# Three of the four low parts of each head's output weights made by GpSimd instead of VectorE

## Chip, cores and metric

The kernel runs on one core of a Trainium2 chip. The metric is the device time of one execution in microseconds (us); lower is better.

## What is computed

One inference step of a two-layer trunk: layer 0 is sliding-window attention, layer 1 an mLSTM block, for a prompt of 1024 tokens (with 16 meta tokens ahead of it) and for 8 short samples of 4 tokens. The change lies in the second layer. Per head (4 heads of width 512) the prompt goes through a chunkwise recurrence, here shortened to its shape:

```
def step(carry, xs):                      # one chunk of one head
    C, n, m = carry                       # C: 512 x 512 state
    s = einsum('td,jd->tj', qc, kc) * w_intra
    num = s @ vc + w_inter * (qc @ C)
    den = sum(s, axis=j) + w_inter * (qc @ n)
    h = num / max(abs(den), exp(-m_t))
    C_new = decay * C + (kc * wk).T @ vc
    n_new = decay * n + sum(wk * kc)
...
h_norm = (h - mean(h)) * rsqrt(var(h) + eps) * head_norm
y = ((sigmoid(o) * h_norm + skip * xc) * silu(z)) @ w_out
```

The sum over heads in `@ w_out` is made head by head: each head adds its 512 rows of `w_out` times its 512 gated channels to the output.

## The kernel before

After a first stage (projections) the kernel runs the cell stage, from about 1612 us to the end, head after head. The text calls the heads 0 to 3; head 0 and head 3 are written out with constants, heads 1 and 2 are two turns of one hardware loop, whose waits use registers. A head has chunks 0 to 8 of the prompt (chunk 0 has the 16 meta tokens, the others 128 each) and one set of samples. Each engine has its own program (`cell_pe`, `cell_dve`, `cell_act`, `cell_gp`, `cell_sp`) and they meet only by semaphores; the order on each engine is written out by hand.

In a chunk `c` TensorE (PE) transposes keys and values (`pre`, L1564), multiplies queries by the state (L1635), makes the rest of the numerator (L1646), then the state's update (L1653). VectorE (DVE) copies the denominator out (L1943), works on it in three tiny instructions (`denominator`, L1853 to L1855), adds the four quarters of the update to the state `cst` (`prompt_state`, L1872), takes the statistics and makes the normed output `hb` (`normed`, L1879 and L1880), which PE transposes (`back`, L1582). PE's update and DVE's addition alternate over two banks of `ps`, so each can hold up the other. From chunk 2 on DVE also updates one sample's state per chunk (`sample_state`, L1811). GpSimd (POOL) makes gates, key weights, queries times weight (`queries`, L1480) and, last in a chunk, one sample's keys (`sequence_keys`, L1498).

The output product at a head's end (`out_part`, L1678) multiplies in single passes, so each weight is split in a high part `whi` (by ScalarE, `w_high`, L1757) and a low part `wlo = wraw - whi`. The head's weights come in four pieces of 128x1024 over three buffers. Their low parts were made by DVE in `w_low` (L1895): pieces 0 to 2 between the sample updates and the denominator of chunks 1 to 3, piece 3 amid the output product, once piece 0's buffer is free. The loads of the pieces, in `cell_sp`, wait on the same semaphore `o_lo` that counts low parts.

Of the kernel before, what the change touches and what calls it, by code (L numbers as in the profile page):

```python
# [20 lines left out]
F32 = mybir.dt.float32  # L21
F32R = mybir.dt.float32r
ALU = mybir.AluOpType
# [25 lines left out]
KT = D // P  # L49
# [48 lines left out]
def due(n):  # L98

    n = n.v if isinstance(n, Idx) else n  # L100
    return max(n, 0) if isinstance(n, int) else n


def wait_apart(eng, sem, n):


    n = n.v if isinstance(n, Idx) else n
    if not isinstance(n, int):
        n = eng.to_reg(n)
        eng.wait_ge(sem, 1)  # L110
    eng.wait_ge(sem, due(n))
# [21 lines left out]
def build(nc, a, o):  # L133
# [3 lines left out]
    def sem(name):  # L137
        if name not in sems:
            sems[name] = nc.alloc_semaphore(name + sem_suffix[0])
        return sems[name]  # L140
# [3 lines left out]
    def sb(name, shape, off, dt=F32):  # L144
        assert BASE + off + 4 * int(np.prod(shape[1:])) <= 229368, name
        return nc.alloc_sbuf_tensor_at("sb_" + name, shape, dt, offset=BASE + off)
# [40 lines left out]
    wraw = [sb(f"wraw{i}", [P, KT * P], WB + i * SLOT) for i in range(NSLOT)]  # L187
    whi = [sb(f"whi{i}", [P, KT * P], WB + (NSLOT + i) * SLOT, F32R) for i in range(NSLOT)]
    wlo = [sb(f"wlo{i}", [P, KT * P], WB + (2 * NSLOT + i) * SLOT, F32R) for i in range(NSLOT)]
# [1139 lines left out]
    def pre_no(c):  # L1329

        return 0 if c == NCH - 1 else c + 1

    def used(h, c):

        return NU * h + (u_tile(c - 2, 3) + 1 if c > 1 else 0)
# [8 lines left out]
    def turn_of(h, c):  # L1344

        return 5 * h + c // 2 if c % 2 == 0 else 4 * h + c // 2
# [101 lines left out]
    def cell_gp(gp, h):  # L1448
        def exponents(c):

            n = ROWN[c]
            if c == NCH - 1:
                gp.wait_ge(sem("head_set"), 4 * h + 4)
                gp.tensor_tensor(ees[:, :], habs[:, :], trism[:, :], ALU.add).then_inc(sem("e_ready"), 1)
                return
            gp.wait_ge(sem("abc_in"), 16 * h + 16)
            gp.wait_ge(sem("w_done"), NCH * h + pre_no(c) - 1)
            if c > 1:
                gp.wait_ge(sem("u_add"), NCH * h + c - 1)
            else:  # L1460
                gp.wait_ge(sem("qs_ready"), NCH * h + pre_no(c))
            gp.tensor_tensor(ee[c % 2][0:n, 0:n], abc[0:n, COL0[c]:COL0[c] + n], tri[0:n, 0:n], ALU.add)\
                .then_inc(sem("e_ready"), 1)

        def queries(c):

            n = ROWN[c]
            if c == NCH - 1:
                gp.wait_ge(sem("smin"), 144 * h + 144)
                w, dst = hws[:, :], qss  # L1470
            else:
                gp.wait_ge(sem(f"chin{c % 2}"), 48 * turn_of(h, c) + 48)
                gp.wait_ge(sem("wint"), NP * h + c + 1)
                gp.wait_ge(sem("u_ready"), used(h, c))
                w, dst = wnt[c % 2][:, 0:n], qs[c % 2]
            if c in (NCH - 1, 0):
                gp.wait_ge(sem("e_ready"), NCH * h + pre_no(c) + 1)
            else:
                gp.wait_ge(sem("kwt_ready"), NP * h + c)
            gp.tensor_tensor(dst[:, :, 0:n], chunk_in(c)[:, 0, :, 0:n],  # L1480
                             w.rearrange("p (a t) -> p a t", a=1).to_broadcast([P, 4, n]), ALU.mult)\
                .then_inc(sem("qs_ready"), 1)

        def spread_queries():

            wait_apart(gp, sem("qs_ready"), NCH * h + 1)
            wait_apart(gp, sem("sn_full"), h)
            gp.tensor_copy(diagonal(qz), qss[:, :, :].rearrange("p k (b t) -> p b k t", b=DECB)).then_inc(sem("qz_ready"), 1)

        def sequence_keys(b):  # L1490

            wait_apart(gp, sem("k3_lo"), 2 * h + 1)
            if b < DECB - 1:
                wait_apart(gp, sem("qs_ready"), NCH * h + pre_no(b + 2) + 1)
            else:
                wait_apart(gp, sem("kwt_ready"), NP * h + NP)
            wait_apart(gp, sem("u_ready"), samp_used(h, b))
            gp.tensor_scalar(kwz[b % 2][:, :], k3[:, :].bitcast(F32), blkm[0:SR, b:b + 1], None, ALU.mult).then_inc(sem("kwz_ready"), 1)  # L1498

        def gated(c):  # L1500

            n, u = ROWN[c], ub[c % 2]
            gb = gates_of(c)[1]
            wait_gates(gp, h, c)
            gp.wait_ge(sem("u_mul"), NCH * h + c + 1)
            gp.tensor_tensor(u[:, :, 0:n], u[:, :, 0:n], gb[:, :, 0:n], ALU.add).then_inc(sem("u_add"), 1)

        def put_low(c):

            n, u = ROWN[c], ub[c % 2]  # L1510
            gp.wait_ge(sem("uh_done"), NCH * h + c + 1)
            cols = slice(COL0[c], COL0[c] + n)
            gp.tensor_tensor(ul[:, :, cols], u[:, :, 0:n], uh[:, :, cols].bitcast(F32), ALU.subtract).then_inc(sem("ul_done"), 1)  # L1513

        def weighted_keys(c):

            n = ROWN[c]
            gp.wait_ge(sem(f"chin{c % 2}"), 48 * turn_of(h, c) + 48)
            gp.wait_ge(sem(f"chw{c % 2}"), 16 * turn_of(h, c) + 16)
            if c == 0:  # L1520
                gp.wait_ge(sem("num9"), h)
            else:
                gp.wait_ge(sem("ns_ready"), NP * h + c)
            gp.tensor_tensor(kwt[:, :, 0:n], chin[c % 2][:, 1, :, 0:n],
                             chw[c % 2][:, 0:n].rearrange("p (a t) -> p a t", a=1).to_broadcast([P, 4, n]), ALU.mult)\
                .then_inc(sem("kwt_ready"), 1)

        exponents(NCH - 1)
        queries(NCH - 1)
        spread_queries()  # L1530
        exponents(0)
        queries(0)
        for c in range(NP):
            if c >= 1:
                gated(c - 1)
            if c + 1 < NP:
                exponents(c + 1)
            weighted_keys(c)
            if c >= 1:
                put_low(c - 1)  # L1540
            if c + 1 < NP:
                queries(c + 1)
            if c >= 1:
                sequence_keys(c - 1)
        gp.wait_ge(sem("kwz_ready"), DECB * h + DECB)
        for c in (NP - 1, NCH - 1):
            gated(c)
            put_low(c)

    def cell_pe(pe, h):  # L1550
# [131 lines left out]

        pe.wait_ge(sem("ul_done"), NCH * h + NP)
        pe.wait_ge(sem("c_done"), NU * h + NU)
        pe.wait_ge(sem("o_lo"), 4 * h + 1)
        out_part(0, (0, 1))
        out_part(1, (0, 1))
        back(NCH - 1)
# [2 lines left out]
        for i in range(2):  # L1691
            out_part(i, (2,)).then_inc(sem("o_full"), 1)
        for i in range(2, KT):
            pe.wait_ge(sem("o_lo"), 4 * h + i // 2 + 1)
            pe.wait_ge(sem("o_done"), KT * h + i - 1)
            out_part(i, (0, 1, 2)).then_inc(sem("o_full"), 1)

# [83 lines left out]
    def cell_dve(dve, h):  # L1781
# [108 lines left out]
            dve.tensor_tensor(u[:, :, 0:n], pm[1][:, :].rearrange("p (k t) -> p k t", k=4)[:, :, 0:n], ga[:, :, 0:n], ALU.mult)\  # L1890
                .then_inc(sem("u_mul"), 1)

        def w_low(j):
            dve.wait_ge(sem("o_hi"), due(4 * h + j + 1))
            dve.tensor_tensor(wlo[j % 3][:, :], wraw[j % 3][:, :], whi[j % 3][:, :].bitcast(F32), ALU.subtract)\  # L1895
                .then_inc(sem("o_lo"), 1)


        if isinstance(h, int) and h == 0:
# [25 lines left out]
        for c in range(NP):  # L1925
            n, r = ROWN[c], c % 2
            if c == 0:
                dve.wait_ge(sem("cst_out"), 16 * h)
            if c > 0:
                put(c - 1)  # L1930
            score_low(c)
            value_low(c)
            if c > 1:
                sample_state(c - 2, 0)
                sample_state(c - 2, 1)
            key_low(c)
            if c > 1:
                sample_state(c - 2, 2)
                sample_state(c - 2, 3)
            if 0 < c < 4:  # L1940
                w_low(c - 1)
            small(c + 1)
            done(dve.tensor_copy(cs[0:n, r, 0:1], SM[0:n, 0:1]))  # L1943
            dve.sem_inc(sem("small_read"), 1)
            denominator(c)
            prompt_state(c, 0)
            prompt_state(c, 1)
            statistics(c)
            prompt_state(c, 2)
            prompt_state(c, 3)  # L1950
            normed(c)
            if c + 1 < NP:
                scores(c + 1)
            key_state(c)
# [15 lines left out]
        for i in range(KT):  # L1970
            dve.wait_ge(sem("o_full"), KT * h + i + 1)
            dve.tensor_tensor(v3(x1T[:, i, :]), ps[i % 2][:, :, 0:GRP], v3(x1T[:, i, :]), ALU.add).then_inc(sem("o_done"), 1)  # L1972
            if i == 1:
                w_low(3)
        dve.wait_ge(sem("o_done"), KT * h + KT)
        assert step[0] == CELL_STEPS, step[0]

# [554 lines left out]
```

## Time and profile before

| | |
|---|---|
| time, median of 3 runs | 2410.4 us (2406.17 to 2413.91) |
| profiled execution: its time, its span | 2409.14 us, 2407.4 us |
| PE busy, share of span | 2197.8 us, 91% |
| DVE busy | 1120.1 us, 47% |
| ACT busy | 711.0 us, 30% |
| POOL busy | 497.0 us, 21% |
| DVE `wlo` in the cell stage (L1895), 16 of them | 24.1 us, 1504 ns each |

Shares of busy time are means over stages with different limits. In the timeline a row has the start, the duration and what ended the engine's idle time before it. Granted clock 1.00 is TensorE's 2.4 GHz level and 0.50 its 1.2 GHz level.

### The profile page before, as it was taken

To read this page: it belongs to the slowest core of one execution; us is meant where nothing else is said; L and a number is where in the kernel's file an instruction comes from. 1 tells how busy PE (TensorE), PEld (TensorE's weight loads), DVE (VectorE), ACT (ScalarE), POOL (GpSimd) and SP (SyncE) were. 2 spreads that over 40 slices of the span, in tenths; PEclk is the share of its full clock that TensorE was granted. 3 is DMA by queue.
4 is the path that set the end of the run, shared out by engine and by line. 5 is a ranking of instruction groups with operands and counts; after the bars stand their busy time and mean duration, and the time that the engine had idled before them with its cause. 6 is when DMAs were issued, how large, how long until landed. Compare 5 with 4: busy or idle time off the path is not lost. (4 is left out here: it accounts for less than half of the span.)

```text
span 2407.4 us, 34739 instructions
## 1 busy us (share of the span) xinstructions
PE 2197.8 (91%) x12991; PEld 1902.7 (79%) x12991; DVE 1120.1 (47%) x1906; ACT 711.0 (30%) x1497; POOL 497.0 (21%) x464
## 2 busy tenths in 40 slices
PE   5999979968999999999999999928998998999997
PEld 4999967737999989998998999815686676667667
DVE  6222348733554305512451354037736844853863
ACT  3115658821133313322332232113303312311320
POOL 3000026601420001100010010004503512521430
PEclk8999979957999999999999999968998988988999
DMA  6621021002331332232123222237853861754661
GB/s 207 83 79 36 27 61 51 1 26 96 118 90 63 118 109 63 81 127 83 63 81 136 74 82 98 84 80 236 254 167 91 254 178 54 244 173 121 192 203 74
DMA packets 307072, 268.43 MB, mean 112 GB/s; under 512 B 60642, under 2 KB 252610, under 8 KB 306831
## 3 DMA queue, kind: packets, MB, share of 16 engines
q1 hardware_dynamic: 293034, 217.48, 30.2%
q10 hardware_dynamic: 13880, 48.77, 6.2%
q8 instruction: 109, 1.79, 0.3%
q14 instruction: 49, 0.40, 0.1%
HBM read 164.75 MB, written 102.40 MB: 111 GB/s over the span
## 5 line engine op out<-in xcount | busy, mean ns | idle before, releaser
L380 DVE TENSOR_TENSOR sb_wlo<-sb_wraw,sb_whi 128x1024 fp32r<-128x1024 f32 x100 | 143.2, 1432 | 278.8 <-ACT sb_whi L375 272.1
L396 PE MATMUL ps<-sb_h1h,sb_whi 128*128 128x360 f32 x1152 | 253.7, 328 | 3.8 <-issue 3.8
L375 ACT ACTIVATE sb_whi<-sb_wraw 128x1024 fp32r<-128x1024 f32 x100 | 105.7, 1058 | 512.8 <-PE ps L396 443.4
L396 PE MATMUL ps<-sb_h1l,sb_whi 128*128 128x360 f32 x1152 | 252.5, 327 | 0.0
L396 PE MATMUL ps<-sb_h1h,sb_wlo 128*128 128x360 f32 x1152 | 252.2, 327 | 0.0
L396 PEld LDWEIGHTS ps<-sb_h1h,sb_whi 128*128 128x128 f32 x1152 | 198.9, 188 | 6.5 <-issue 6.3
L396 PEld LDWEIGHTS ps<-sb_h1h,sb_wlo 128*128 128x128 f32 x1152 | 199.7, 188 | 0.0
L396 PEld LDWEIGHTS ps<-sb_h1l,sb_whi 128*128 128x128 f32 x1152 | 199.4, 188 | 0.0
L948 POOL COPY sb_ctail<-sb_xr 128x3 f32<-128x3 f32 (+1 forms) x16 | 3.0, 188 | 708.4 <-DVE sb_xr L1081 708.4
L1635 PE MATMUL pm<-sb_cst,sb_qs 128*128 128x512 f32 x256 | 135.5, 611 | 1.0 <-issue 0.9
L396 PE MATMUL ps<-sb_hh,sb_whi 128*128 128x360 f32 x480 | 117.4, 353 | 15.8 <-DVE sb_hl L417 12.6
L1054 ACT ACTIVATE sb_st<-ps 128x1080 f32<-128x1080 f32 x48 | 51.5, 1072 | 226.8 <-PE ps L396 226.8
L1811 DVE SCALAR_TENSOR_TENSOR sb_scs<-sb_scs,sb_hbc,ps 128x512 f32<-128x512 f32 x128 | 94.4, 744 | 29.8 <-PE ps L1591 29.7
L396 PE MATMUL ps<-sb_hl,sb_whi 128*128 128x360 f32 x480 | 107.4, 333 | 0.0
L396 PE MATMUL ps<-sb_hh,sb_wlo 128*128 128x360 f32 x480 | 106.7, 331 | 0.0
L396 PEld LDWEIGHTS ps<-sb_hh,sb_whi 128*128 128x128 f32 x480 | 85.5, 194 | 24.8 <-issue 9.8
L1678 PE MATMUL ps<-sb_uh,sb_whi 128*128 128x360 f32 x384 | 92.7, 336 | 11.8 <-POOL sb_ul L1513 11.8
L1972 DVE TENSOR_TENSOR sb_x1T<-ps,sb_x1T 128x1080 f32<-128x1080 f32 x32 | 41.1, 1283 | 127.8 <-PE ps L1678 127.8
L1638 PEld LDWEIGHTS ps<-sb_nst,sb_qs 128*128 128x128 f32 x256 | 48.9, 191 | 62.6 <-issue 62.6
L1678 PE MATMUL ps<-sb_uh,sb_wlo 128*128 128x360 f32 x384 | 91.3, 332 | 0.0
L1678 PE MATMUL ps<-sb_ul,sb_whi 128*128 128x360 f32 x384 | 91.1, 332 | 0.0
L1872 DVE SCALAR_TENSOR_TENSOR sb_cst<-sb_cst,sb_hbc,ps 128x512 f32<-128x512 f32 x128 | 89.4, 739 | 0.6 <-issue 0.6
(394 smaller groups left out, 4726.6 us busy)
## 6 DMA issues: line engine op xcount, KB each, us to landing
sb_scs<-state_mlstm_c SPq DMA_DIRECT2D x32, 1024.0 KB, 5.5
sample_mlstm_c<-sb_scs SPq DMA_DIRECT2D x32, 1024.0 KB, 4.4
sb_wraw<-mlstm_w_in SPq DMA_DIRECT2D x48, 512.0 KB, 3.8
sb_wraw<-swa_w_in SPq DMA_DIRECT2D x20, 512.0 KB, 3.8
scratch_ga<-sb_st ACTq DMA_DIRECT2D x16, 540.0 KB, 2.7
scratch_gb<-sb_st ACTq DMA_DIRECT2D x16, 540.0 KB, 3.7
scratch_v<-sb_st ACTq DMA_DIRECT2D x16, 540.0 KB, 2.7
scratch_q<-sb_st ACTq DMA_DIRECT2D x16, 540.0 KB, 2.7
```

The costliest lines, as they stand in the source:

```text
L375: act.activation(whi[q][:, :], wraw[q][:, :], ACT.Copy).then_inc(sem("w_hi"), 1)
L380: dve.tensor_tensor(wlo[q][:, :], wraw[q][:, :], whi[q][:, :].bitcast(F32), ALU.subtract)\
L396: last = pe.matmul(ps[s][:, g, 0:GRP], w[:, kk, c * P:(c + 1) * P], x[:, kk, g * GRP:(g + 1) * GRP], start=(kk == 0 and i == 0), stop=(kk ...
L948: gp.tensor_copy(dst[:, 0:CW - 1], x[:, NPR:XPR])
L1054: act.activation(v3(st[b][:, 0, :]), ps[c][:, :, 0:GRP], ACT.Copy, scale=(MD ** -0.5 if i // 4 == 2 else 1.0)).then_inc(sem("qkv_ev"), 1)
L1635: pe.matmul(pm[0][0:n, :], qs[r][:, k, 0:n], cst[:, k, :], start=(k == 0), stop=False)
L1638: pe.matmul(SM[0:n, 0:1], qs[r][:, k, 0:n], nst[:, k:k + 1], start=(k == 0), stop=False)
L1678: last = pe.matmul(ps[i % 2][:, g, 0:GRP], w[:, k, c * P:(c + 1) * P], x[:, k, g * GRP:(g + 1) * GRP], start=(k == 0 and t == 0), stop=(k ...
L1811: dve.scalar_tensor_tensor(scs[b % 2][:, k, :], scs[b % 2][:, k, :], hbc[:, 1, NP + b:NP + b + 1], U_[u % 2], ALU.mult, ALU.add).then_inc( ...
L1872: ins = dve.scalar_tensor_tensor(cst[:, k, :], cst[:, k, :], hbc[:, 1, c:c + 1], U, ALU.mult, ALU.add)
L1972: dve.tensor_tensor(v3(x1T[:, i, :]), ps[i % 2][:, :, 0:GRP], v3(x1T[:, i, :]), ALU.add).then_inc(sem("o_done"), 1)
```

## The change

GpSimd makes pieces 0 to 2 at the end of its chunks 1 to 3, DVE keeps piece 3, and PE waits for three low parts at once before the output product.

```diff
@@ cell_gp
+        def weight_low(j):
+            wait_apart(gp, sem("o_hi"), 4 * h + j + 1)
+            wait_apart(gp, sem("o_full"), KT * h)
+            gp.tensor_tensor(wlo[j][:, :], wraw[j][:, :], whi[j][:, :].bitcast(F32), ALU.subtract).then_inc(sem("o_lo"), 1)
...
             if c >= 1:
                 sequence_keys(c - 1)
+            if c in (1, 2, 3):
+                weight_low(c - 1)
@@ cell_pe
-        pe.wait_ge(sem("o_lo"), 4 * h + 1)
+        pe.wait_ge(sem("o_lo"), 4 * h + 3)
...
         for i in range(2, KT):
-            pe.wait_ge(sem("o_lo"), 4 * h + i // 2 + 1)
+            if i == 6:
+                pe.wait_ge(sem("o_lo"), 4 * h + 4)
@@ cell_dve
-        def w_low(j):
-            dve.wait_ge(sem("o_hi"), due(4 * h + j + 1))
-            dve.tensor_tensor(wlo[j % 3][:, :], wraw[j % 3][:, :], whi[j % 3][:, :].bitcast(F32), ALU.subtract)\
-                .then_inc(sem("o_lo"), 1)
+        def last_low():
+            dve.wait_ge(sem("o_hi"), 4 * h + 4)
+            dve.wait_ge(sem("o_lo"), 4 * h + 3)
+            dve.tensor_tensor(wlo[0][:, :], wraw[0][:, :], whi[0][:, :].bitcast(F32), ALU.subtract).then_inc(sem("o_lo"), 1)
...
-            if 0 < c < 4:
-                w_low(c - 1)
...
             if i == 1:
-                w_low(3)
+                last_low()
```

On POOL, chunk 1 of head 0, the order before is this (L1480 are the queries of chunk 2, L1498 the sample's keys; `sb_kwz` is their tile):

```order
L1524 TENSOR_TENSOR sb_nums<-sb_chin_191,sb_headsum 128x512
L1513 TENSOR_TENSOR sb_ul<-sb_ub_243,sb_uh 128x4x16
L1480 TENSOR_TENSOR sb_qs_228<-sb_chin_190,sb_wnt_212 128x512
L1498 ISA
L1498 TENSOR_SCALAR sb_kwz_236<-sb_k_232,sb_blkm 96x512
L1506 TENSOR_TENSOR sb_ub_244<-sb_ub_244,sb_chga_193 128x512
```

and this is what stands there now:

```order
L1524 TENSOR_TENSOR sb_nums<-sb_chin_191,sb_headsum 128x512
L1513 TENSOR_TENSOR sb_ul<-sb_ub_243,sb_uh 128x4x16
L1480 TENSOR_TENSOR sb_qs_228<-sb_chin_190,sb_wnt_212 128x512
L1498 ISA
L1498 TENSOR_SCALAR sb_kwz_236<-sb_k_232,sb_blkm 96x512
L1531 TENSOR_TENSOR sb_wlo_71<-sb_wraw_65,sb_whi_68 128x1024
L1506 TENSOR_TENSOR sb_ub_244<-sb_ub_244,sb_chga_193 128x512
```

One instruction came in, between the sample's keys and the gate (L1506) that opens the next chunk on POOL.

On DVE, chunk 2 of head 0, before (L1811 adds to a sample's state, L1943 opens the denominator):

```order
L1811 SCALAR_TENSOR_TENSOR sb_scs_205<-sb_scs_205,sb_hbc,ps 128x512 x2
L1818 SCALAR_TENSOR_TENSOR sb_kl_220<-ps,sb_hcol,sb_kh_218 128x512
L1811 SCALAR_TENSOR_TENSOR sb_scs_205<-sb_scs_205,sb_hbc,ps 128x512 x2
L1895 TENSOR_TENSOR sb_wlo_72<-sb_wraw_66,sb_whi_69 128x1024
L1943 COPY sb_cs<-ps 128x1
L1853 SCALAR_TENSOR_TENSOR sb_cs<-sb_cs 128x1
L1854 TENSOR_TENSOR sb_cs<-sb_cs,sb_hcol 128x1
```

and now (the same lines stand 6 to 8 lines further down in the file):

```order
L1819 SCALAR_TENSOR_TENSOR sb_scs_205<-sb_scs_205,sb_hbc,ps 128x512 x2
L1826 SCALAR_TENSOR_TENSOR sb_kl_220<-ps,sb_hcol,sb_kh_218 128x512
L1819 SCALAR_TENSOR_TENSOR sb_scs_205<-sb_scs_205,sb_hbc,ps 128x512 x2
L1949 COPY sb_cs<-ps 128x1
L1861 SCALAR_TENSOR_TENSOR sb_cs<-sb_cs 128x1
L1862 TENSOR_TENSOR sb_cs<-sb_cs,sb_hcol 128x1
```

The low part left the place ahead of the denominator; nothing else moved.

## Rows read from the trace of the kernel before

**Rows 1.** Chain that ended last, head 2, chunk 3: start, us, piece

```profile
2063.00 0.94 DVE sb_cs L1853
```

**Rows 2.** Timeline of DVE, head 2: start, us, instruction, [idle before <-releaser]

```profile
2029.47 1.98 DVE L1895 TENSOR_TENSOR sb_wlo<-sb_wraw,sb_whi 128x1024 fp32r<-128x1024 f32 x1
2033.80 0.16 DVE L1943 COPY sb_cs<-ps 128x1 f32<-128x1 f32 x1 [2.34 <-PE pm L1646]
2034.10 0.16 DVE L1853 SCALAR_TENSOR_TENSOR sb_cs<-sb_cs 128x1 f32<-128x1 f32 x1
...
2047.07 1.51 DVE L1895 TENSOR_TENSOR sb_wlo<-sb_wraw,sb_whi 128x1024 fp32r<-128x1024 f32 x1
...
2063.00 0.93 DVE L1853 SCALAR_TENSOR_TENSOR sb_cs<-sb_cs 128x1 f32<-128x1 f32 x1
...
2068.32 0.15 DVE L1879 TENSOR_TENSOR sb_cs<-sb_cs 128x1 f32<-128x1 f32 x1
...
2076.77 0.16 DVE L1943 COPY sb_cs<-ps 128x1 f32<-128x1 f32 x1 [0.17 <-PE pm L1646]
...
2116.28 0.16 DVE L1943 COPY sb_cs<-ps 128x1 f32<-128x1 f32 x1 [0.17 <-PE pm L1646]
```

**Rows 3.** Timeline of POOL (GpSimd), head 2, chunks 1 to 3

```profile
2028.20 0.32 POOL L1506 TENSOR_TENSOR sb_ub<-sb_ub,sb_chga 128x64 f32<-128x64 f32 x1 [13.75 <-DVE sb_ub L1890]
...
2030.33 1.30 POOL L1513 TENSOR_TENSOR sb_ul<-sb_ub,sb_uh 128x64 fp32r<-128x64 f32 x1
...
2033.02 1.56 POOL L1498 TENSOR_SCALAR sb_kwz<-sb_k,sb_blkm 96x512 fp32r<-96x512 f32 x1 [0.16 <-POOL sb_qs L1480]
...
2047.66 2.35 POOL L1498 TENSOR_SCALAR sb_kwz<-sb_k,sb_blkm 96x512 fp32r<-96x512 f32 x1 [0.16 <-POOL sb_qs L1480]
...
2061.67 2.25 POOL L1480 TENSOR_TENSOR sb_qs<-sb_chin,sb_wnt 128x512 f32<-128x512 f32 x1 [0.88 <-DMA sb_chin<-scratch_v]
2064.22 1.56 POOL L1498 TENSOR_SCALAR sb_kwz<-sb_k,sb_blkm 96x512 fp32r<-96x512 f32 x1 [0.31 <-POOL sb_qs L1480]
```

**Rows 4.** Timeline of PE, head 2, behind the third low part

```profile
2065.20 0.50 PE L1653 MATMUL ps<-sb_vh,sb_kh 128*128 128x512 f32 x1 [2.05 <-DVE sb_cst L1872]
```

**Rows 5.** Groups of POOL instructions by shape: xcount | busy us, mean ns

```profile
L952 POOL TENSOR_TENSOR sb_xml<-sb_xr,sb_xmh 128x1040 fp32r<-128x1040 f32 x16 | 41.5, 2594 | 0.0
```

**Rows 6.** Timelines of POOL and DVE, chunk 1 of heads 0, 1 and 3

```profile
1651.10 1.57 POOL L1498 TENSOR_SCALAR sb_kwz<-sb_k,sb_blkm 96x512 fp32r<-96x512 f32 x1 [0.17 <-issue]
...
1651.83 0.16 DVE L1854 TENSOR_TENSOR sb_cs<-sb_cs,sb_hcol 128x1 f32<-128x1 f32 x1
...
1836.98 1.56 POOL L1498 TENSOR_SCALAR sb_kwz<-sb_k,sb_blkm 96x512 fp32r<-96x512 f32 x1 [0.16 <-POOL sb_qs L1480]
...
1839.96 0.16 DVE L1853 SCALAR_TENSOR_TENSOR sb_cs<-sb_cs 128x1 f32<-128x1 f32 x1
...
2224.55 1.56 POOL L1498 TENSOR_SCALAR sb_kwz<-sb_k,sb_blkm 96x512 fp32r<-96x512 f32 x1 [0.16 <-issue]
...
2225.12 0.16 DVE L1853 SCALAR_TENSOR_TENSOR sb_cs<-sb_cs 128x1 f32<-128x1 f32 x1 [0.15 <-DVE sb_cs L1943]
```

**Rows 7.** Timelines of DVE and PE, head 3, chunks 3, 4 and 7

```profile
2252.83 0.15 DVE L1943 COPY sb_cs<-ps 128x1 f32<-128x1 f32 x1
...
2255.14 0.50 PE L1653 MATMUL ps<-sb_vh,sb_kh 128*128 128x512 f32 x1 [1.84 <-DVE sb_cst L1872]
...
2268.01 0.16 DVE L1943 COPY sb_cs<-ps 128x1 f32<-128x1 f32 x1 [0.17 <-PE pm L1646]
...
2306.42 0.16 DVE L1943 COPY sb_cs<-ps 128x1 f32<-128x1 f32 x1 [0.17 <-PE pm L1646]
```

**Rows 8.** Windows of 1 us, head 3: busy us (x) of PE, PEld, DVE, ACT, POOL, granted clock, DMA

```profile
2257.00:2258.00 1.00, 1.00 (x6) 0.94 (x5) 1.00 (x2) 0.41 (x2) 0.00 (x0) 0.50 0.25 45
```

**Rows 9.** Timelines of PE and POOL, head 2, inputs of chunk 8

```profile
2119.50 1.03 PE L1564 MATMUL ps<-sb_ident,sb_chin 128*128 128x128 f32 x8
...
2119.51 1.28 POOL L1480 TENSOR_TENSOR sb_qs<-sb_chin,sb_wnt 128x512 f32<-128x512 f32 x1 [4.28 <-DMA sb_chin<-scratch_v]
```

## Prediction

> **What bounds the kernel now.** I read the page first: PE is busy for 91% of the span, but that is a mean over stages, and the change touches only the cell stage, four heads of some 195 us. So I read the chain that ended last there. It hops between PE and DVE in every chunk: PE's query and update products, then DVE's denominator and the first quarter of the state, then PE's update again. One of its pieces is a DVE instruction on a 128x1 column that takes 0.94 us [rows 1]. The timeline of DVE tells why that is odd. The reader is to see three things in it [rows 2]. First, in chunk 1 DVE makes a low part (2029.47, 1.98 us) and then idles 2.34 us until PE ends the numerator: that low part costs the chain nothing. Second, the denominator's copy L1943 gives the beat of the chunks: 2076.77 to 2116.28 is three chunks without low part, 39.51 us or 13.17 each; 2033.80 to 2076.77 is three that hold the second and third low part, 42.97 us. Third, L1853 takes 0.16 us at 2034.10 and 0.93 at 2063.00, behind the third low part. The timeline of POOL gives the reason [rows 3]: POOL's queries began at 2061.67, took 2.25 us instead of 1.28 [rows 9] and ended at 2063.92; L1853 ended at 2063.93. DVE's low part and POOL's product kept each other out, and then POOL kept DVE's tiny instruction out until its own end. In chunk 1 it is the same the other way: POOL's L1513 on 64 columns took 1.30 us beside DVE's low part, where L1506 on as many took 0.32 [rows 3]. So two engines share something when both read two tensors from SBUF. L1872, L1811 and the statistics read one tensor there and the other in PSUM, and show no such lengthening. This is what the change has to be judged by, since it puts the longest such instruction on POOL.
>
> **What it removes.** Per head, 3.46 us at most (42.97 - 39.51) [rows 2]; at least the 1.51 us of the second low part plus the 0.77 us that L1853 lost (0.93 - 0.16), 2.28 us. In chunk 2 of heads 1 and 2 the sample's keys L1498 now start right at the denominator (2047.66 [rows 3] against 2047.07 plus L1943 and L1853), and L1854, with two tensors in SBUF, will meet them. How long L1498 keeps others out is bounded by head 3: L1853 starts 0.57 us behind the start of L1498 and takes 0.16 [rows 6], so for less than 0.57 us. I take 0.4 of that off and get 3.1 us per head, 12.4 in all (the written-out heads 0 and 3 lose less there, but have shorter chunks).
>
> The Trainium skill, "SBUF — State Buffer", section "Who interferes with whom", says that whichever of the two engines starts first gets the shared pair "for the whole instruction". For L1498, with one tensor input, head 3's row says otherwise: L1853 would have had to wait a microsecond there. By the page the sum would come out about 2 us higher, 2409; by the row it stays.
>
> Heads 0 and 3 have one more thing to get back. PE waits 1.84 us behind the third low part, and the granted clock then falls to 0.50, the 1.2 GHz level [rows 7, 8]. L1943 to L1943 takes 15.18 us there; in head 2 the same stretch is 14.07 (2063.00 less 0.30 to 2076.77 [rows 2]), and head 3's plain chunk is 12.80 (2268.01 to 2306.42, three of them [rows 7]), 0.37 shorter than head 2's. So the fall costs 15.18 - 14.07 + 0.37 = 1.5 us. Heads 1 and 2 had the longer wait (2.05 [rows 4]) without a fall. With the wait gone, two falls go: 3.0 us. Gross gain: 15.4 us.
>
> **What it adds.** A 128x1024 subtraction of two SBUF tensors on POOL. The nearest row is L952, same form, 1040 columns, 2.59 us [rows 5]; for 1024, 2.55 us. POOL has room for it: it follows L1498 (kwz), and POOL's next gate waits for DVE, so at the end of its own chunk it delays nobody on POOL. But for 2.4 us (until some 0.15 us before its end, since L1853, 0.16 us long, ended together with L1480 above) DVE can't run L1853, L1854, L1879 or L1840, all with two SBUF tensors. So the question is where these fall.
>
> Chunk 1: without DVE's low part beside it, L1513 takes 0.32 instead of 1.30, and all behind it on POOL moves up 0.98. In head 2, L1498 goes from 2033.02 to 2032.04, ends at 2033.6 [rows 3], and the low part runs from 2033.6 to 2036.1. PE's numerator hasn't moved, so L1853 comes at 2034.10 [rows 2], is kept out until 2036.0 and delays the first quarter of the state, for which PE waits: 1.9 us on the chain. In head 0, L1498 moves from 1651.10 to 1650.12 and the low part starts at 1651.66; L1854 comes at 1651.83 [rows 6]: it loses by 0.17 us and waits 2.2. Head 3 alike: low part from 2225.1, L1853 at 2225.12: 2.2. Head 1's PE is later: low part from 1837.5 to 1840.1, L1853 at 1839.96 [rows 6]: nothing. Sum 6.3 us; bounds 0 (DVE is first each time) and 8.8 (all four heads).
>
> Chunk 2: the low part runs from 2049.2 to 2051.7 in head 2. L1879 comes 4.4 us after the end of L1853 (2063.93 and 2068.32 [rows 2]), which ends at about 2047.8, plus the 0.4 that L1854 waits: 2052.6. Free: 0, but only by a microsecond.
>
> Chunk 3: POOL's queries wait for their load (0.88 us for chin [rows 3]). That load hangs on a store issued before the second low part's place, so it doesn't come earlier, while DVE does, by about 2.6 us. In head 2: queries at 2061.67 for 1.28, L1498 at 2063.25, low part from 2064.8 to 2067.3. L1879 comes at 2068.32 - 2.6 = 2065.7 [rows 2], waits 1.5 us, and with it `hb` and PE's transposes; in the trace those follow within 0.3 us, so 1.3 of it counts, and 1.4 in head 1. Head 0 is a tie (L1879 against the start of the low part): 0 or 2.1, I take 1. In head 3 L1879 is first and L1840 waits, 0.3. Sum 4.0; bounds 0 and 7.2.
>
> New waits of PE: 2.4 to 2.6 us in chunk 1 of three heads (0.2 to 0.7 now, plus 1.9 to 2.2). Two of four waits of 1.84 to 2.05 us brought a clock fall; I take one and a half falls at 1.5 us: 2.2. Bounds 0 and 4.5, 12 if each long wait of chunk 1 and 3 brings one.
>
> Loads: in head 2 the last chunk's keys landed just as PE and POOL wanted them [rows 9], and chunks at 13.17 us from chunk 2 on press the queues one or two chunks longer. I take 1 us in all; bounds 0 and 3 in each of two heads.
>
> Edits at nothing: PE's wait for three low parts comes behind all nine chunks, five of them after the last of these; `last_low` is the same instruction at the same place; the two waits in `weight_low` are long satisfied, hidden by L1498; the loads of the pieces wait for the previous head's fourth low part, as before.
>
> **Sum.** -12.4 - 3.0 + 6.3 + 4.0 + 2.2 + 1.0 = -1.9 us. The profiled execution took 2409.1, 1.3 below the median of 2410.4 and within the runs shown; 2407.
>
> **Rivals.** (a) The forecast, chance 0.56: the time that DVE is spared comes back as DVE's tiny instructions waiting for POOL; 2401 to 2415. (b) No collision that counts, 0.25: POOL is some tenths later than I reckon, or lets DVE in early; 15.4 us less is 2394, or 2397 with the clock falls left. For it: margins of 0.02 and 0.17 us in heads 3 and 0. Against: half a microsecond in head 2. (c) Slower, 0.13: PE's waits in chunk 1 bring TensorE's clock down. Collisions in all heads (8.8 + 7.2), nothing back from the old falls, and a fall at each of eight places (12) make 2409.1 - 12.4 + 16 + 12 = 2425. It decides once four falls stand beside all the collisions: 2409.1 - 12.4 + 16 + 6 = 2419. Against: head 1 has no collision in chunk 1. (d) The loads become the bound, 0.06: chunks keep the old pace from landing to landing and the gain is gone without any collision; 2409.
>
> **Numbers.** A measurement here tells 0.3%, 7.2 us: below 2403.2 is faster, above 2417.6 slower. (b) is all faster, and a small part of (a); (c) mostly slower. Faster 0.27, same 0.60, slower 0.13. Range 2396 to 2418: down to (b), up to the edge of (c).
>
> **What would show it.** In the changed profile: no 128x1024 DVE instruction in chunks 1 to 3; POOL's at about 2.55 us, following L1498 at once; L1853 or L1854 of chunk 1 lengthened to about 2 us in heads 0, 2 and 3 and not in head 1; L1879 of chunk 3 lengthened in heads 1 and 2; chunk 2's denominator following the sample update directly; whether the clock stays at 1.00 from chunk 1 on. The prediction is wrong if L1853 keeps 0.16 us while POOL's low part runs, or if the clock falls again and again.

## The result and the profile after

The changed kernel takes 2421.3 us (median), the kernel before on the same chips 2412.1: a ratio of 1.0035, 95% interval [1.0022, 1.0048]. It is slower by some 8.5 us, and above the range that I gave. The profiled execution has a span of 2416.1 us, where before's has 2407.4. The difference arises in chunks 1 to 3 of the four heads, whose beats (denominator's copy to denominator's copy) are 11.0 us longer in sum; elsewhere the changed kernel's profiled execution is 2.3 us shorter, by tenths of a us in single chunks and by how long the clock stands at 0.50 behind a head's last chunk, which differs between the executions.

POOL's new group, from the groups of instructions of the changed kernel, cell stage (count, busy us, mean ns):

```profile
L1531 POOL TENSOR_TENSOR sb_wlo<-sb_wraw,sb_whi 128x1024 fp32r<-128x1024 f32 x12 | 28.4, 2365 | 0.0
```

It takes 2.37 us, a little less than the 2.55 that I had from [rows 5]. In all this section the tiny instructions are L1861 and L1862 (before L1853 and L1854), L1887 (before L1879); the denominator's copy is L1949, the update L1660.

This is head 2, chunk 2 in the timeline of the changed kernel, where I had said "free", and under it the copy of the next chunk:

```profile
2053.84 0.16 DVE L1949 COPY sb_cs<-ps 128x1 f32<-128x1 f32 x1 [0.17 <-PE pm L1653]
2054.18 1.57 POOL L1498 TENSOR_SCALAR sb_kwz<-sb_k,sb_blkm 96x512 fp32r<-96x512 f32 x1 [0.16 <-POOL sb_qs L1480]
2054.41 3.66 DVE L1862 TENSOR_TENSOR sb_cs<-sb_cs,sb_hcol 128x1 f32<-128x1 f32 x1
2055.72 2.34 POOL L1531 TENSOR_TENSOR sb_wlo<-sb_wraw,sb_whi 128x1024 fp32r<-128x1024 f32 x1
2059.08 0.79 PE L1660 MATMUL ps<-sb_vh,sb_kh 128*128 128x512 f32 x1 [3.89 <-DVE sb_cst L1880]
...
2072.95 0.16 DVE L1949 COPY sb_cs<-ps 128x1 f32<-128x1 f32 x1 [0.17 <-PE pm L1653]
```

The reader is to see when L1862 starts and when it ends. It starts 0.23 us behind the sample's keys, 1.3 us before the low part, and ends at 2058.07, with the low part (2058.06): it was kept out over both, one behind the other. PE then waits 3.89 us for the first quarter of the state. From copy to copy this chunk is 19.11 us; plain ones are 13.15. Head 1 shows the same 3.66 us and 18.91.

Heads 0 and 3 meet it elsewhere. In the same timeline, head 0 (chunks 1 and 3) and head 3 (chunks 1 and 3):

```profile
1651.10 2.78 DVE L1861 SCALAR_TENSOR_TENSOR sb_cs<-sb_cs 128x1 f32<-128x1 f32 x1 [0.15 <-DVE sb_cs L1949]
1651.51 2.35 POOL L1531 TENSOR_TENSOR sb_wlo<-sb_wraw,sb_whi 128x1024 fp32r<-128x1024 f32 x1
...
1684.63 1.56 POOL L1498 TENSOR_SCALAR sb_kwz<-sb_k,sb_blkm 96x512 fp32r<-96x512 f32 x1 [0.16 <-issue]
1685.12 3.40 DVE L1887 TENSOR_TENSOR sb_cs<-sb_cs 128x1 f32<-128x1 f32 x1
...
2233.45 1.57 DVE L1861 SCALAR_TENSOR_TENSOR sb_cs<-sb_cs 128x1 f32<-128x1 f32 x1 [0.15 <-DVE sb_cs L1949]
...
2264.68 2.57 DVE L1887 TENSOR_TENSOR sb_cs<-sb_cs 128x1 f32<-128x1 f32 x1
```

In heads 0 and 3 the tiny instruction came up to 1.3 us behind the keys' start and 0.2 to 1.0 us ahead of the low part (but for L1861 of head 3, which came when the low part was already running), and each time it came free only with the low part's end. Head 1's L1861 in chunk 1 has 0.39 us, and head 2 goes free there: its denominator comes late, when the low part has just ended:

```profile
2038.59 2.37 POOL L1531 TENSOR_TENSOR sb_wlo<-sb_wraw,sb_whi 128x1024 fp32r<-128x1024 f32 x1
2041.00 0.16 DVE L1861 SCALAR_TENSOR_TENSOR sb_cs<-sb_cs 128x1 f32<-128x1 f32 x1
```

Less the 0.16 (0.15 for L1887) that each takes when free, the waits are 2.62, 0.23, 0 and 1.41 us in chunk 1 of heads 0 to 3, 3.50 twice in chunk 2, 3.25 and 2.42 in chunk 3 of heads 0 and 3: 16.9 us.

The third thing is the clock. In the windows of the changed kernel (busy us and count of PE, PEld, DVE, ACT, POOL, then the granted clock, then DMA) there is a stretch at 0.50, the 1.2 GHz level, behind each of the five longest of those waits:

```profile
1656.00:1658.00 2.00, 2.00 (x7) 1.50 (x6) 1.45 (x5) 0.50 (x2) 0.00 (x0) 0.50 0.00 0
1690.00:1692.00 2.00, 2.00 (x5) 1.00 (x4) 1.33 (x3) 0.00 (x0) 0.49 (x1) 0.50 1.11 344
1862.00:1864.00 2.00, 2.00 (x6) 1.52 (x6) 1.79 (x5) 0.50 (x2) 0.00 (x0) 0.50 0.84 262
2062.00:2064.00 2.00, 2.00 (x12) 2.00 (x11) 1.62 (x3) 0.94 (x2) 0.00 (x0) 0.50 1.07 337
2270.00:2272.00 2.00, 2.00 (x3) 0.93 (x4) 1.18 (x2) 0.92 (x3) 1.83 (x3) 0.50 1.17 293
```

Before had two such stretches in chunks 1 to 3, one of them in [rows 8]. The sixth wait, 1.41 us in head 3, has none behind it. The stretches differ in length: 3 to 4 us at 0.50 in head 0, as in the two of before, and 6 to 7 us in the other three.

### The profile page after: what moved, and what is told of

It is laid out like the page before. It is cut to its first block and busy times, and to the rows that moved or that the text cites. A ratio compares the mean times of both kernels' runs of the same rounds, so it can differ in the third digit from the quotient of the medians.

```text
span 2416.1 us, 34743 instructions
## 1 busy us (share of the span) xinstructions
PE 2205.7 (91%) x12991; PEld 1907.5 (79%) x12991; DVE 1115.2 (46%) x1894; ACT 711.3 (29%) x1497; POOL 515.0 (21%) x476
## 5 line engine op out<-in xcount | busy, mean ns | idle before, releaser
L1642 PE MATMUL pm<-sb_cst,sb_qs 128*128 128x512 f32 x256 | 141.2, 635 | 0.7 <-issue 0.7
```

Source lines behind the costliest of these rows:

```text
L1642: pe.matmul(pm[0][0:n, :], qs[r][:, k, 0:n], cst[:, k, :], start=(k == 0), stop=False)
```

## Experiments

Where nothing else is said, an edit is made to the changed kernel, and the ratio is to the kernel before, run on the same chip. An added line moves the lines below it by one, a split one by two.

**Low part in name only.** GpSimd's three low parts have 8 of 1024 columns and VectorE makes none of them; the products with the other columns use what lay in the buffer.

```diff
-            gp.tensor_tensor(wlo[j][:, :], wraw[j][:, :], whi[j][:, :].bitcast(F32), ALU.subtract).then_inc(sem("o_lo"), 1)
+            gp.tensor_tensor(wlo[j][:, 0:8], wraw[j][:, 0:8], whi[j][:, 0:8].bitcast(F32), ALU.subtract).then_inc(sem("o_lo"), 1)
```

> Left out: the low parts of pieces 0 to 2 but for 8 of 1024 columns, on both engines (the output product reads what lies in the buffers). It shows the most that taking them off DVE can bring. Theory A: 12 to 15 us below before, ratio 0.994 to 0.995, and the same as the run in which the low part waits for the first quarter. Rival (loads bound): ratio 0.999 to 1.001 here too.

Measured 0.9934 [0.9911, 0.9956]. 0.0066 of 2412 us is 15.9 us (10.6 to 21.5 by the interval): this is what taking the three low parts off VectorE is worth, and my 15.4 stands. So 1.0035 - 0.9934, 24.4 us, give or take 6, is what they cost on POOL, where I had 13.5. Head 2, chunk 2, in the timeline of this run:

```profile
2037.55 1.56 POOL L1498 TENSOR_SCALAR sb_kwz<-sb_k,sb_blkm 96x512 fp32r<-96x512 f32 x1 [0.16 <-POOL sb_qs L1480]
2037.84 0.41 DVE L1862 TENSOR_TENSOR sb_cs<-sb_cs,sb_hcol 128x1 f32<-128x1 f32 x1
```

The same instruction meets the same keys 0.29 us behind their start and is through in 0.41. It ends 0.70 us behind the keys' start; less its own 0.16 the keys alone hold VectorE for 0.54 us, within my bound of 0.57. That was right; what was wrong was to price the keys and the low part apart.

**A gap between the keys and the low part.** GpSimd waits for its own keys to be written before it starts the low part.

```diff
         def weight_low(j):
             wait_apart(gp, sem("o_hi"), 4 * h + j + 1)
+            wait_apart(gp, sem("kwz_ready"), DECB * h + j + 1)
```

> Edit: GpSimd's low part waits for the end of the sample's keys L1498 (kwz) in front of it, 0.2 to 0.3 us of pause; nothing is left out. Theory A (back to back POOL instructions keep DVE out as one: L1862 of head 2's chunk 2 waited 3.66 us behind kwz and low part together): in chunk 2 of heads 1 and 2 L1862 gets in between, 0.5 to 0.7 us instead of 3.66; in head 0's chunk 1 L1861 takes 0.16 instead of 2.78. L1887 of chunk 3 may still wait about 2.3 us. Time 4 to 9 us below the change, ratio to before 0.998 to 1.002. Theory B (DVE waits for any low part that starts within about a microsecond, pause or not): L1862 stays at 3.4 to 3.7 us, the time stays at 1.003 to 1.005.

Measured 0.999 [0.9973, 1.0006]. The timeline, head 2, chunk 2 and then chunk 3:

```profile
2048.54 1.58 POOL L1498 TENSOR_SCALAR sb_kwz<-sb_k,sb_blkm 96x512 fp32r<-96x512 f32 x1 [0.16 <-POOL sb_qs L1480]
2048.79 0.47 DVE L1863 TENSOR_TENSOR sb_cs<-sb_cs,sb_hcol 128x1 f32<-128x1 f32 x1
2050.26 2.40 POOL L1532 TENSOR_TENSOR sb_wlo<-sb_wraw,sb_whi 128x1024 fp32r<-128x1024 f32 x1
...
2066.52 1.77 DVE L1888 TENSOR_TENSOR sb_cs<-sb_cs 128x1 f32<-128x1 f32 x1
```

The low part starts 0.14 us behind the keys' end where it had started 0.03 before it, and 3.66 us become 0.47: the wait of chunk 2 lives on the two following each other directly, which the semaphore breaks. It isn't the whole loss. A tiny instruction that comes while the low part itself runs still waits, as L1888 does here (1.77) and in head 1 (1.87), and L1863 in head 3's chunk 1 (2.33). The same happens to L1862 in head 0's chunk 1: 2.10, where 0.16 was expected.

**Start behind the denominator.** GpSimd starts the low part only when VectorE has written the first quarter of the chunk's state.

```diff
+            wait_apart(gp, sem("c_done"), NU * h + u_tile(j + 1, 0) + 1)
```

> Edit: GpSimd's low part waits until DVE has added the first quarter of this chunk's state (c_done), that is past L1861 and L1862; nothing is left out. From the first quarter's end to L1887 there are about 3.1 us, the low part takes 2.4. Theory A (the whole loss is DVE's two-SBUF-input instructions waiting for POOL, and the clock falls behind those waits): no L1861, L1862 or L1887 above 0.4 us, no clock fall in chunks 1 to 4, all four heads 3 to 5 us shorter than before: 12 to 15 us below before, ratio 0.994 to 0.995. Rival (loads or PE become the bound when DVE is spared): the small instructions are short and the time is still within 3 us of before, ratio 0.999 to 1.001.

Measured 0.9961 [0.9943, 0.9979]: better than before. The middle is short of the 0.994 to 0.995 expected, the interval isn't; but long waits and a clock fall, which were expected to be gone, are there. Head 2 in its timeline, chunk 3, and then the denominator of chunk 4:

```profile
2060.22 1.56 POOL L1498 TENSOR_SCALAR sb_kwz<-sb_k,sb_blkm 96x512 fp32r<-96x512 f32 x1 [0.31 <-POOL sb_qs L1480]
2061.75 2.36 POOL L1532 TENSOR_TENSOR sb_wlo<-sb_wraw,sb_whi 128x1024 fp32r<-128x1024 f32 x1
2062.53 1.60 DVE L1888 TENSOR_TENSOR sb_cs<-sb_cs 128x1 f32<-128x1 f32 x1
...
2072.98 1.28 POOL L1480 TENSOR_TENSOR sb_qs<-sb_chin,sb_wnt 128x512 f32<-128x512 f32 x1 [1.85 <-DMA sb_chin<-scratch_v]
2072.99 1.28 DVE L1863 TENSOR_TENSOR sb_cs<-sb_cs,sb_hcol 128x1 f32<-128x1 f32 x1
```

The denominator waits nowhere in chunks 1 to 3, but for 0.3 us at the keys in two places. But in chunk 3 the keys come late and push the low part onto the statistics' last product L1888, which waits in all heads (it takes 2.04, 1.81, 1.60, 2.59 us), with a clock fall behind the last. In heads 0 and 2 something more follows, which I call the echo: in the next chunks the denominator falls on POOL's queries L1480, whose start hangs on a load. Chunks 4 to 7 are 13.7 to 13.9 us instead of 12.8 in head 0, chunks 4 to 6 14.1 to 14.4 instead of 13.2 in head 2. Heads 1 and 3 waited as long and have no echo, so being late isn't enough for it.

**One tensor instead of two.** GpSimd copies the raw weight into the low part's place and leaves the subtraction of the high part out.

```diff
-            gp.tensor_tensor(wlo[j][:, :], wraw[j][:, :], whi[j][:, :].bitcast(F32), ALU.subtract).then_inc(sem("o_lo"), 1)
+            gp.tensor_copy(wlo[j][:, :], wraw[j][:, :]).then_inc(sem("o_lo"), 1)
```

> Left out: the subtraction; GpSimd copies the raw weights into the low part at the same place, so it reads one SBUF tensor where the change reads two. Theory A with a hold that lasts as long as POOL reads: the copy is shorter (some 1.0 to 1.6 us for 1024 columns) but still holds DVE out for most of it: L1862 of chunk 2 in heads 1 and 2 takes 1.5 to 2.5 us, time between before and the change, ratio 1.000 to 1.003. Rival (only an instruction with two inputs on POOL keeps DVE out; kwz alone let L1853 in after less than 0.57 us): L1861, L1862 and L1887 at 0.16 to 0.7 us and the time near the version with nothing to wait for, ratio 0.994 to 0.997.

Measured 0.9954 [0.9937, 0.997]. Head 2, chunk 2 in its timeline:

```profile
2044.01 1.57 POOL L1498 TENSOR_SCALAR sb_kwz<-sb_k,sb_blkm 96x512 fp32r<-96x512 f32 x1 [0.16 <-POOL sb_qs L1480]
2044.25 1.03 DVE L1862 TENSOR_TENSOR sb_cs<-sb_cs,sb_hcol 128x1 f32<-128x1 f32 x1
2045.54 1.03 POOL L1531 CAST sb_wlo<-sb_wraw 128x1024 fp32r<-128x1024 f32 x1
```

The copy takes 1.03 us for as many columns, so size and kind change together here. L1862 ends at 2045.28, before the copy starts and 1.27 us behind the keys' start, 0.57 later than with nothing long behind them. The expectation had 1.5 to 2.5 us for this wait by theory A and 0.16 to 0.7 by its rival; neither came. That one tensor isn't harmless shows in head 3, chunk 1, of the same timeline:

```profile
2221.09 1.04 POOL L1531 CAST sb_wlo<-sb_wraw 128x1024 fp32r<-128x1024 f32 x1
2221.13 1.02 DVE L1861 SCALAR_TENSOR_TENSOR sb_cs<-sb_cs 128x1 f32<-128x1 f32 x1 [0.15 <-DVE sb_cs L1949]
```

L1861 is kept out for the whole copy, and in chunk 1 of heads 0 and 2 it ends with the copy too (0.49 and 0.61 us). So POOL needs no second SBUF tensor to keep VectorE's two-tensor instruction out; the copy costs less because it is shorter. No clock fall is left in chunks 1 to 3.

**One piece at a time.** Only the second, only the first, only the third low part on GpSimd; the other two stay in VectorE's old place, and the load of piece 3 waits for three low parts. For the second:

```diff
-            if c in (1, 2, 3):
+            if c in (2,):
                 weight_low(c - 1)
...
+            if c in (1, 3):
+                w_low(c - 1)
             small(c + 1)
```

> Only the second low part (chunk 2) is made by GpSimd; the first and third stay on VectorE. Theory of back-to-back holding: in heads 1 and 2 the denominator still meets the sample's keys and the low part behind them, one wait of 3.7 us each with a clock fall behind it, so the beat from chunk 2 to 3 is about 19 us there (14.2 before), while the beat from chunk 1 to 2 loses 1.4 us in all four heads: -6 + 9.5 = +3.5 us, ratio 1.0015. Rival (the prediction's step, chunk 2 is free): no wait over 0.5 us in chunk 2, -6 us, ratio 0.9975.

Measured 1.0008 [0.9995, 1.002], where "free" asked for 0.9975 and the theory for 1.0015. The timeline of head 2, chunk 2:

```profile
2046.95 3.66 DVE L1862 TENSOR_TENSOR sb_cs<-sb_cs,sb_hcol 128x1 f32<-128x1 f32 x1
2048.25 2.33 POOL L1531 TENSOR_TENSOR sb_wlo<-sb_wraw,sb_whi 128x1024 fp32r<-128x1024 f32 x1
```

It is 3.66 us again, in heads 1 and 2, and nowhere else. The clock falls behind both.

> Only the first low part (chunk 1) is made by GpSimd. Both the prediction's step and the theory now say that VectorE saves nothing (it idled there) and that its denominator waits in chunk 1: by the prediction 1.9 to 2.2 us in heads 0, 2 and 3 (+6.3 us), by the theory fitted to the changed kernel 2.6, 0.2, 0 and 1.4 us in heads 0 to 3, with one clock fall of some 1.5 us (+5.7 us). Ratio 1.002 to 1.003. Which heads wait tells them apart. Rival: no price at all (0.9995 to 1.0005), so that all the loss of the change sits in chunks 2 and 3.

Measured 1.0044 [1.0027, 1.006], 10.6 us, more than either account. Head 0, chunk 1 and chunk 5, and head 3, chunk 1, of this run:

```profile
1651.80 2.94 DVE L1861 SCALAR_TENSOR_TENSOR sb_cs<-sb_cs 128x1 f32<-128x1 f32 x1 [0.15 <-DVE sb_cs L1956]
...
1712.73 1.29 POOL L1480 TENSOR_TENSOR sb_qs<-sb_chin,sb_wnt 128x512 f32<-128x512 f32 x1 [1.02 <-DMA sb_chin<-scratch_v]
1712.88 1.15 DVE L1861 SCALAR_TENSOR_TENSOR sb_cs<-sb_cs 128x1 f32<-128x1 f32 x1 [0.15 <-DVE sb_cs L1956]
...
2240.76 1.61 DVE L1861 SCALAR_TENSOR_TENSOR sb_cs<-sb_cs 128x1 f32<-128x1 f32 x1 [0.15 <-DVE sb_cs L1956]
```

The heads that wait are 0 and 3, none in 1 and 2. The rest is in head 0: chunk 2 has a clock fall that before doesn't have (its beat is 15.98 us instead of 13.85), and chunks 4 to 7 have the echo, denominators of 1.1 us at the queries.

> Only the third low part (chunk 3) is made by GpSimd. VectorE is spared 1.5 us and the 0.8 us that its denominator lost to the queries, in four heads, and the two old clock falls go: -12.2 us. By the prediction's step waits of 4.0 us in all come at the statistics' last product: -8 us, ratio 0.9966. By what the changed kernel shows (3.3 and 2.4 us in heads 0 and 3, none in 1 and 2, each with a clock fall): -3.5 us, ratio 0.9985.

Measured 0.9978 [0.9965, 0.9991], between the two accounts and compatible with both. L1887 waits in head 0 only (1.65 us), with no clock fall behind it, so neither account has the right heads. The queries meet the denominator twice in head 3 and once each in heads 0 and 1 (1.0 to 1.3 us), and head 2 has a clock fall in chunk 2, where VectorE still makes the low part. The three ratios add up to 1.0008 + 0.0044 - 0.0022 = 1.0030, beside 1.0035 for the whole change.

**Halves.** Each of GpSimd's low parts in two instructions of 512 columns, with no wait between them; and then in 768 and 256.

```diff
-            gp.tensor_tensor(wlo[j][:, :], wraw[j][:, :], whi[j][:, :].bitcast(F32), ALU.subtract).then_inc(sem("o_lo"), 1)
+            for q in (slice(0, 512), slice(512, 1024)):
+                ins = gp.tensor_tensor(wlo[j][:, q], wraw[j][:, q], whi[j][:, q].bitcast(F32), ALU.subtract)
+            ins.then_inc(sem("o_lo"), 1)
```

> The changed kernel, with each of GpSimd's low parts made in two instructions of 512 columns that follow each other with no wait between. Theory 1 (VectorE is kept out for the length of one instruction and can get in at the end of each): the denominator's wait of 3.66 us in chunk 2 of heads 1 and 2 ends with the first half, at about 2.4 us, and the long waits of heads 0 and 3 lose up to 1.2 us each; fewer clock falls; ratio 0.998 to 1.001. Theory 2 (GpSimd takes up its next instruction before the last has ended, so that VectorE is kept out through a whole row of them that follow with no wait): the waits stay at 3.6 to 3.9 us and the ratio at 1.003 to 1.005.

Measured 0.9968 [0.9956, 0.9979], better than either theory. Head 2, chunk 2, and then head 0, chunk 1; the two halves are one row (x2), 1.28 us each:

```profile
2043.22 1.58 POOL L1498 TENSOR_SCALAR sb_kwz<-sb_k,sb_blkm 96x512 fp32r<-96x512 f32 x1 [0.16 <-POOL sb_qs L1480]
2043.47 1.28 DVE L1864 TENSOR_TENSOR sb_cs<-sb_cs,sb_hcol 128x1 f32<-128x1 f32 x1
...
1648.55 2.51 POOL L1532 TENSOR_TENSOR sb_wlo<-sb_wraw,sb_whi 128x512 fp32r<-128x512 f32 x2
1649.07 0.78 DVE L1863 SCALAR_TENSOR_TENSOR sb_cs<-sb_cs 128x1 f32<-128x1 f32 x1 [0.15 <-DVE sb_cs L1951]
1649.89 1.19 DVE L1864 TENSOR_TENSOR sb_cs<-sb_cs,sb_hcol 128x1 f32<-128x1 f32 x1
```

In head 0 VectorE gets one instruction in between the halves (it ends at 1649.85, and the first half ends 1.28 behind 1648.55, at 1649.83), and the next waits for the second half: theory 1's picture. In head 2 L1864 is free at 2044.75, at the keys' end and before either half, which neither theory had. That holds for an instruction that comes early: L1889 in head 3's chunk 3 comes 1.47 us behind the keys' start, just ahead of the first half, and is free only at that half's end (1.36 us). No wait above 1.4 us is left, and no clock fall in chunks 1 to 3.

> The changed kernel with each of GpSimd's low parts in two instructions of 768 and 256 columns, with no wait between. In the run with two of 512 columns the denominator of chunk 2, caught 0.25 us behind the start of the sample's keys, came free after 1.28 us, at the keys' end; in the changed kernel with one of 1024 columns it came free only at the low part's end, after 3.66 us. Theory (a long instruction behind the keys takes the place over before VectorE gets in, from some size between 512 and 1024 columns): either 1.3 us again (then the point lies above 768 columns) or the keys' rest and 768 columns, 1.3 + 1.8 = 3.1 us. Time: ratio 0.997 in the first case, 1.000 to 1.002 in the second. Rival (what counts is that there are two instructions): 1.3 us and 0.997.

Measured 1.0017 [0.9999, 1.0034]. Head 1, chunk 2 of its timeline:

```profile
1853.17 1.59 POOL L1498 TENSOR_SCALAR sb_kwz<-sb_k,sb_blkm 96x512 fp32r<-96x512 f32 x1 [0.16 <-POOL sb_qs L1480]
1853.42 3.12 DVE L1864 TENSOR_TENSOR sb_cs<-sb_cs,sb_hcol 128x1 f32<-128x1 f32 x1
1854.73 2.48 POOL L1532 TENSOR_TENSOR sb_wlo<-sb_wraw,sb_whi 128x768 fp32r<-128x768 f32 x2
```

3.12 us, to 1856.54, which is the end of the 768 columns (1.82 us from 1854.73). Head 0's chunk 1 shows the same (3.22 us, to the end of the 768). So it is not the count of instructions: behind the keys, 512 columns let an early VectorE instruction in first and 768 don't.

**The low part ahead of the keys.** As in "start behind the denominator", and besides GpSimd makes the low part before the sample's keys of the same chunk. The window was read off the timeline: from the first quarter of the state to L1887 there is room for 2.4 us of low part, and the keys, which hold VectorE only at their start, come then.

```diff
         def weight_low(j):
             wait_apart(gp, sem("o_hi"), 4 * h + j + 1)
+            wait_apart(gp, sem("c_done"), NU * h + u_tile(j + 1, 0) + 1)
...
+            if c in (1, 2, 3):
+                weight_low(c - 1)
             if c >= 1:
                 sequence_keys(c - 1)
-            if c in (1, 2, 3):
-                weight_low(c - 1)
```

> GpSimd makes the low part ahead of the sample's keys of the same chunk, and only once VectorE has written the first quarter of the chunk's state. Theory (two-input instructions of both engines keep each other out for their whole length, and the sample's keys for some 0.4 us at their start): the low part of 2.4 us then lies between the denominator and the statistics' last product, 4.1 us later, and the keys come in front of that product instead of it. All long waits of VectorE's tiny instructions (16.9 us in the changed kernel, seven of them above 1 us) and the five clock falls in chunks 1 to 3 go; ratio 0.993 to 0.995, like the run with 8 columns. Rival: what the run with the later start alone had left (waits of 1.6 to 2.6 us at the statistics' last product in chunk 3 of all heads, and chunks of 13.8 to 14.3 us behind them because the queries of the next chunks meet the denominator) does not hang on where the low part stands; then 0.996 again. Second rival: the keys, 2.4 us later, are missed by TensorE's sample update: chunks of 15 us, ratio above 1.000.

Measured 0.9923 [0.9906, 0.9941], 2393.7 us: the fastest kernel here, 18.6 us better than before by its ratio, and level with the run that makes only 8 columns. Head 2, chunk 2 in its timeline, and the window of head 2's chunks 1 to 3:

```profile
2037.07 0.16 DVE L1863 TENSOR_TENSOR sb_cs<-sb_cs,sb_hcol 128x1 f32<-128x1 f32 x1
2038.31 2.40 POOL L1532 TENSOR_TENSOR sb_wlo<-sb_wraw,sb_whi 128x1024 fp32r<-128x1024 f32 x1 [1.66 <-DVE sb_cst L1881]
2040.69 1.56 POOL L1498 TENSOR_SCALAR sb_kwz<-sb_k,sb_blkm 96x512 fp32r<-96x512 f32 x1
2041.35 0.15 DVE L1888 TENSOR_TENSOR sb_cs<-sb_cs 128x1 f32<-128x1 f32 x1
```
```profile
2023.00:2066.00 43.00, 41.36 (x209) 27.51 (x208) 34.35 (x76) 15.00 (x50) 27.95 (x21) 1.00 0.63 194
```

L1863 is through before the low part, L1888 comes 0.66 us behind the keys' start, and both have their 0.16. The clock is 1.00 throughout; the other heads' windows say the same. One long one, of 1.07 us, is left, in chunk 3 of head 3.

Two controls. First, an edit to the kernel before: only the keys of chunks 1 to 3 are put behind the first quarter of the state.

```diff
+            if c in (1, 2, 3):
+                wait_apart(gp, sem("c_done"), NU * h + u_tile(c, 0) + 1)
             if c >= 1:
                 sequence_keys(c - 1)
```

> The kernel before, with VectorE making all low parts, and only the sample's keys of chunks 1 to 3 held back on GpSimd until VectorE has written the first quarter of the chunk's state. It tells what of the gain of the version with the low part ahead of the keys comes from the keys' later place alone. Theory (the low part's place made that gain): no change, 0.999 to 1.001, since in the kernel before the keys kept VectorE out only for some tenths. Rival: the keys in the denominator's way are a good part of the loss; 0.997 or less.

Measured 0.999 [0.9981, 1.0]: the keys' place alone gives 0.1%, by the interval at most 0.2%. Its head 0 has the echo too, in chunks 4 to 6 (0.86, 1.19 and 1.06 us), though no wait is above 1 us ahead of it; without that the keys' place might give a little more. Second, low part ahead of the keys and in halves:

> Both remedies together: GpSimd's low part ahead of the sample's keys, once the chunk's first quarter of the state is written, and in two instructions of 512 columns. If what is left of waits in the version with the first remedy (one of 1.1 us in the profiled execution) is all that the halves can take away, this gives the same as that version, 0.992 to 0.993. Rival: the second instruction ends later by 0.15 us and brings the keys' start onto the statistics' last product in more places; 0.994 to 0.995.

Measured 0.9929 [0.9905, 0.9953]: the same as without halves; where nothing collides, cutting gives nothing.

## Why the prediction was wrong

The mechanism, VectorE's tiny instructions waiting for POOL, was the right one in the main; the sign of the sum was wrong, because two terms were too small, the waits and the clock falls. In the order of its steps:

- **"Two engines share something when both read two tensors from SBUF".** Too narrow. The run with the copy shows POOL keeping VectorE out with one tensor (1.02 us), and the line of L1498 at 2047.66 in [rows 3] had shown the other way round: the keys, one tensor, took 2.35 us instead of 1.56 beside VectorE's low part. No term hangs on it, but it hid how alike the keys and the low part are.
- **"What it removes", 15.4 us.** Right: 15.9 by the run with 8 columns.
- **"Chunk 2 ... Free: 0, but only by a microsecond".** This is the step that failed. The sum had the keys hold L1854 for 0.4 us and the low part begin after that, with L1854 gone. Heads 1 and 2 measured 3.50 us each, 7.0 in all: with 1024 columns directly behind the keys, VectorE isn't let in when the keys let go. The gap run (0.47 us) shows that it needs the two to follow each other directly, the run with only the second piece (3.66 again) that it needs nothing else of the change. I said that L1854 would meet the keys and took the duration from a row, head 3's [rows 6], in which nothing large followed them; that was the choice to doubt. The Trainium skill, "SBUF — State Buffer", "Who interferes with whom", which I set aside here for L1498 because of that row, gives whichever engine issues first the shared pair of ports for the whole instruction. With the low part already running the trace agrees (head 3's L1861, 1.57 us, to the low part's end). For the keys alone the runs still say otherwise (0.70 of 1.56 us); with the low part directly behind them VectorE fared worse than by the rule (3.89 us from the keys' start).
- **Chunk 1, 6.3 us.** 4.3 measured (2.62, 0.23, 0, 1.41). Heads 0 and 3 collide and head 1 doesn't, as predicted; head 2 doesn't either, because its denominator came 3.94 us behind the keys' start where [rows 2, 3] had 1.08. The copies of chunks 0 and 1 of head 2 are 15.0 to 15.2 us apart in some profiled runs and 17.2 to 17.4 in others. A price that hangs on half a microsecond there is one execution's, not the kernel's.
- **Chunk 3, 4.0 us.** 5.7 measured, in heads 0 and 3 (3.25, 2.42) instead of 1 and 2 (none). That chunk 2's delay had moved DVE out of the way is likely, not shown: with the gap, which takes that delay away, heads 1 and 2 do wait (1.87, 1.77 for L1888), but in the run with only the third piece, which has no such delay either, they don't.
- **Clock, one and a half falls, 2.2 us.** The count was off, five and not one and a half. 24.4 less the 16.9 us of waits is 7.5, or 1.5 us each, the price that I had from [rows 7, 8]; but that is a remainder between two ratios, good to some 6 us. The beats of the profiled execution, less the plain beat and the wait, say more: 1.6 and 1.2 us for the two falls of head 0, 2.3, 2.5 and 3.0 for those of heads 1, 2 and 3, whose stretches at 0.50 are about twice as long; 10.5 in all. So the price was right for the short kind only. In the changed kernel the waits of 2.4 to 3.5 us all had a fall behind them, those below 1.7 had none. My count came from PE's waits of 1.84 and 2.05 us, shorter than what the collisions made (3.89 in chunk 2), and in that middle it goes either way: a PE wait of 1.78 brought a fall in the run with only the first piece, one of 1.96 none in the run with only the second.
- **Loads, 1.0 us.** Nothing to be seen of it.

With the remainder for the falls, the waits were 6.6 us above their terms, the falls 5.3, the loads 1.0 below and the gain 0.5 above: -1.9 + 6.6 + 5.3 - 1.0 - 0.5 = +8.5. Of the rivals, (c) came nearest. Its mechanism, the clock, is a third of the loss (7.5 of 24.4 us; by the beats 10.5 of 27.4), not its main part, and it put the collisions into chunks 1 and 3. The five falls are past the four from which it was to decide.

What stays open is why 768 or 1024 columns behind the keys keep VectorE out and 512 don't, and why with a copy behind them VectorE comes free at 1.27 us instead of 0.70. Open is too what decides whether the echo comes: the changed kernel has waits of 2.6 and 3.3 us in head 0 and none behind them (chunks 4 to 7 at 12.8 us). The rows show the order in which VectorE got in, not who decides it.

## What to carry to other kernels

Before a long instruction on SBUF tensors goes to GpSimd, write down when VectorE's tiny two-tensor instructions come, and start it by a semaphore just behind one of them, with the next further away than it is long; work that comes "behind the last instruction of its engine" is in a place that nobody chose. Here moving the same instruction cost 8.5 us in the one place and gained 18.6 in the other, two lines apart and behind a semaphore. If there is no such window, cut it into pieces of about a microsecond; two of 1.28 us each gave 0.9968. And price what follows a short hold directly together with it, and read the granted clock behind each wait that it makes.

## What the hardware showed that I had not expected

- How long one VectorE instruction (two SBUF tensors) that comes 0.23 to 0.29 us behind the start of GpSimd's keys is kept out depends on what GpSimd has next. Counted from the keys' start (1.56 to 1.59 us long) it is through at 0.70 to 0.72 us with 8 columns or a gap behind them, 1.27 with a copy of 1024 columns, 1.53 with a subtraction of 512, 3.37 with one of 768, and 3.9 with one of 1024.
- A GpSimd instruction with one SBUF tensor keeps VectorE's two-tensor instruction out as well: 1.02 us beside a copy of 1.04 us.
- In some runs the denominator also falls on POOL's queries in later chunks, 0.7 to 1.1 us of wait each time, up to four chunks long, with no GpSimd work added there. It came behind collisions (the late start, the first piece alone) and once without a long one (the keys' later place), and stayed away behind the longest.
